# Down matmuls by pairs of experts, value products in halves, and a first mixer that starts with index scores and selection

## The reference, cut to what matters

```python
# layer 0 mixer: pool branch and sparse attention (DSA)
u, q, k, v, qi, ki, wi = jnp.split(hn @ w_in, ...)          # 512,512,128,128,256,64,4 columns
a_out = pool_mix(concat(pool_hist, u), ...)                 # windows 2,4,8,16, then one 128x128 product each
s_idx = sum over 4 index heads of relu(qi . ki) * wi        # index scores
sel   = top_k(where(admitted, s_idx, NEG_INF), n_sel)       # 128 keys (prompt), 72 (sample)
b_out = softmax over the selected keys, 8 heads             # 'bthd,bshd', then p @ v
y     = concat(a_out, b_out) @ w_out
# layer 1 mixer: stick-breaking attention (8 heads) and differential attention (4 heads)
# every layer: mixture of experts, 16 experts, each token goes to 2 of them
for e in range(16):
    hid = silu(x @ w1[e]) * (x @ w3[e])                     # 1024 -> 512
    y = y + gate[:, e:e + 1] * (hid @ w2[e])                # 512 -> 1024
```

## Time and profile before

| | us |
|---|---|
| median of 3 runs | 1469.23 (1467.95 to 1471.14) |
| the profiled execution | 1469.25 |
| its span in the trace | 1467.3 |
| PE busy in the span | 1286.9 (88%) |
| DVE, ACT, POOL busy | 469.3, 290.7, 165.4 |

### The profile page before, as it was taken

The page is one execution under the profiler, slowest core; times in us unless marked ns, Lnnn a source line. Parts: engine busy times, 40 slices in busy tenths (PEclk is TensorE's granted clock), DMA queues, the critical chain, the costliest instruction groups (busy, mean ns, idle before and its releaser), DMA issues.

```text
span 1467.3 us, 27763 instructions
## 1 busy us (share of the span) xinstructions
PE 1286.9 (88%) x11991; PEld 825.1 (56%) x11991; DVE 469.3 (32%) x1130; ACT 290.7 (20%) x703; POOL 165.4 (11%) x216
## 2 busy tenths in 40 slices
PE   6999789959999999948998799989877999999960
PEld 3454345548777777714444444444537777777740
DVE  3057873251000000025346651274542000000007
ACT  2122423210000000012345530242210000000013
POOL 0133100010000000020112221110001000000014
PEclk8997979969999999978999799999877999999995
DMA  9400100069999999772002201030038999999744
GB/s 287 129 10 5 59 1 29 15 230 348 372 371 382 380 379 363 293 240 101 22 15 77 107 15 43 29 119 15 29 102 300 385 375 383 381 381 363 306 136 151
DMA packets 69320, 283.55 MB, mean 193 GB/s; under 512 B 19181, under 2 KB 20253, under 8 KB 61002
## 3 DMA queue, kind: packets, MB, share of 16 engines
q1 hardware_dynamic: 56190, 237.94, 43.9%
q0 software_dynamic: 9216, 31.11, 6.0%
q10 hardware_dynamic: 3788, 12.65, 2.2%
HBM read 257.20 MB, written 24.48 MB: 192 GB/s over the span
## 4 chain that ended last, share of the span: by engine, by line
PE 75%; DVE 11%; issue 6%; DMA 2%; ACT 2%; POOL 2%; POOLq 0%; ACTq 0%; DVEq 0%; SPq 0%
PE bank L1058 24%; PE bank L781 15%; PE bank L1070 14%; PE bank L984 8%; PE bank L931 2%; PE bank L814 2%; PE bank L1043 2%; PE bank L900 2%; DVE slot L1546 1%; POOL slot L1985 1%; DVE h L1846 1%; PE bank L909 1%; DVE stats L1545 1%; PE bank L804 1%; DVE stats L1451 1%
## 5 line engine op out<-in xcount | busy, mean ns | idle before, releaser
L1058 PE MATMUL bank<-arena,slot 128*64 128x96 f32 x8192 | 351.4, 248 | 4.5 <-issue 4.4
L1058 PEld LDWEIGHTS bank<-arena,slot 128*64 128x64 f32 x8192 | 343.6, 138 | 11.0 <-issue 8.2
L781 PE MATMUL bank<-slot,xT 128*128 128x512 f32 x512 | 243.8, 633 | 1.1 <-issue 0.9
L1070 PE MATMUL bank<-slot,arena 128*96 128x512 f32 x512 | 227.4, 597 | 2.4 <-ACT arena L1345 2.4
L781 PEld LDWEIGHTS bank<-slot,xT 128*128 128x128 f32 x512 | 102.3, 205 | 122.9 <-issue 122.3
L1070 PEld LDWEIGHTS bank<-slot,arena 128*96 128x96 f32 x512 | 80.8, 163 | 126.8 <-issue 123.3
L1830 DVE TENSOR_TENSOR arena<-arena,bank 128x384 f32<-128x384 f32 x32 | 17.7, 554 | 353.8 <-ACT arena L1338 353.8
L984 PE MATMUL bank<-slot,normed 128*128 128x512 f32 x256 | 119.1, 620 | 0.2 <-ACT normed L1308 0.2
L1822 DVE TENSOR_TENSOR arena<-bank,params 128x768 f32<-128x768 f32 x32 | 30.6, 958 | 191.2 <-PE bank L1043 191.2
L1338 ACT ACTIVATE arena<-bank 128x384 f32<-128x384 f32 x32 | 15.7, 491 | 366.2 <-PE bank L1058 366.2
L931 PE MATMUL bank<-arena,slot 128*128 128x64 f32 (+5 forms) x520 | 78.4, 284 | 4.6 <-ACT slot L1247 3.7
(11 more groups left out here) (179 smaller groups left out, 1105.4 us busy)
## 6 DMA issues: line engine op xcount, KB each, us to landing
slot<-in_moe_w SPq DMA_DIRECT2D x96, 2048.0 KB, 13.3
expert_rows<-arena ACTq DMA_DIRECT2D x32, 384.0 KB, 8.6
slot<-in_w_in_odd SPq DMA_DIRECT2D x6, 2048.0 KB, 9.9
slot<-in_w_in_even SPq DMA_DIRECT2D x3, 2048.0 KB, 15.9
slot<-in_w_out_even SPq DMA_DIRECT2D x2, 2048.0 KB, 10.2
normed_rows<-slot POOLq DMA_DIRECT2D x8, 512.0 KB, 2.9
out<-arena POOLq DMA_DIRECT2D x16, 256.0 KB, 2.3
slot<-in_w_out_odd SPq DMA_DIRECT2D x2, 2048.0 KB, 7.9
```

What stands on the lines that cost most here:

```text
L781: last = nc.tensor.matmul(b[o:o + wide, 0:n], xT[:, k, P * t + o:P * t + o + wide], w[:, k, 0:n], start=(k == 0), stop=(k == KC - 1))
L1058: last = nc.tensor.matmul(bank[o:o + 64, b, CAP * m:CAP * m + CAP], weights(w[par])[:, k, at_:at_ + 64], xgT[:, par, k, :], start=(k == 0) ...
L1070: last = nc.tensor.matmul(bank[0:CAP, 6 + j, :], ghid[:, par, m, :], weights(W2[par], 4)[:, m, 512 * j:512 * j + 512], start=(m == 0), sto ...
```

## The change

Three things.

**Down matmuls by pairs.** Two experts' 2 x 96 = 192 rows are six thirds of 32 rows; times two column halves that is 12 pieces. A *wave* takes four of them at once, each in its own group of 32 columns of the array and with its own moving w2, so that a pair takes three waves of 4 x 4 matmuls. The first wave of a pair goes behind the odd expert's up, the other two behind the next even expert's. A wave fills one bank (6 or 7 in turn); ACT copies 128x512 and stores it with two DMAs of 2-KB rows. w2 gets a third buffer (in `xT`), and SP's order of loads changes: at an even expert e, w2(e+1) and w2(e+2) are issued behind w13(e+2), so that w2(14) now stands ahead of w13(15).

```diff
+WAVES = (((0, 0, 0), (0, 1, 0), (0, 2, 0), (0, 0, 1)),          # (expert of the pair, third, half)
+         ((0, 1, 1), (0, 2, 1), (1, 0, 0), (1, 1, 0)),
+         ((1, 2, 0), (1, 0, 1), (1, 1, 1), (1, 2, 1)))
-            def down(l, e, par):
-                for j in range(2):
-                    for m in range(4):
-                        last = nc.tensor.matmul(bank[0:CAP, 6 + j, :], ghid[:, par, m, :],
-                                                weights(W2[par], 4)[:, m, 512 * j:512 * j + 512],
-                                                start=(m == 0), stop=(m == 3))
+            def down(l, p, part):
+                for m in range(4):
+                    for c, (q, third, j) in enumerate(WAVES[part]):
+                        w2 = w2_ring[(2 * p + q) % 3].rearrange("p (k n) -> p k n", k=4)
+                        last = nc.tensor.matmul(bank[QUARTER * c:QUARTER * c + QUARTER, 6 + w % 2, :],
+                                                ghid[:, q, m, QUARTER * third:QUARTER * third + QUARTER],
+                                                w2[:, m, 512 * j:512 * j + 512], start=(m == 0), stop=(m == 3))
...
                     up(l, e, e % 2)
-                    if e > 0:
-                        down(l, e - 1, (e - 1) % 2)
-                down(l, NE - 1, (NE - 1) % 2)
+                    if e % 2:
+                        down(l, e // 2, 0)
+                    elif e > 0:
+                        down(l, e // 2 - 1, 1)
+                        down(l, e // 2 - 1, 2)
+                down(l, NE // 2 - 1, 1)
+                down(l, NE // 2 - 1, 2)
...
+                    w2_ring_load(l, 2)
+                    for e in range(NE):
+                        if e + 2 < NE:
+                            sp.wait_ge(up_done[l], e + 1)
+                            w13_load(l, e + 2, e % 2)
+                        if e >= 2 and e % 2 == 0:
+                            for done in (e - 2, e - 1):
+                                if done + 3 < NE:
+                                    sp.wait_ge(down_done[l], last_wave(done))
```

**Value products in halves.** For the 128-row tiles of DSA and stick-breaking each matmul becomes two, with 64 columns of probabilities as weights, in the two halves of the array:

```diff
+                    wide = r if w == P else min(r, 64)
                     for i, (vb, kr) in enumerate(blocks):
-                        last = nc.tensor.matmul(out[0:r, w * hd:w * hd + w], probT[0:kr, n % 2, i, 0:r],
+                        for o in range(0, r, wide):
+                            last = nc.tensor.matmul(out[o:o + wide, w * hd:w * hd + w],
+                                                    probT[0:kr, n % 2, i, o:o + wide],
```

```diff
+    dsa(0, "q")
+    dsa(0, "kT")
+    out.append(("us",))
+    dsa(1, "kT", "qiT")
+    dsa(0, "qT")
+    dsa(1, "ix0", "ix1", "ix2", "ix3")
+    out.append(("S", 1, 0, 8))
+    dsa(2, "kv", "ki")
+    out.append(("S", 1, 8, 16))
+    dsa(1, "q")
+    out.append(("u", 0))
...
+    for t in range(2):
+        merged(extra, {(t, hd): [("S", t + 2, 2 * hd, 2 * hd + 2)] for hd in range(8)})
+    merged(extra, {(2, hd): [("S", 4, hd, hd + 1 if hd < 7 else 9)] for hd in range(8)})
...
+                   (0, 3): project("dsa", 4, "cache"), (0, 4): [("u", 1)], (0, 5): project("dsa", 4, "kv4"),
...
+                   (3, 3): [("Ub", 3), ("y", 0, 0, 0)], (3, 4): [("O", "dsa", 2)],
...
-            w_out_load(w_out_even, OUT_EVEN, (lambda: sp.wait_ge(bank_filled, number[("us",)] + 1),
+            w_out_load(w_out_even, OUT_EVEN, (lambda: sp.wait_ge(bank_filled, number[("u", 3)] + 1),
```

More of the change, by code:

```diff
@@ L1 @@
+import itertools
 import concourse.bass as bass
@@ L122, in schedule @@
-    extra = {}
[L123 to L132, removed]
@@ L133, in schedule, with turn_in, dsa @@
-    merged(extra, {(0, 0): project("dsa", 1, "qT"), (0, 1): [("Uv", 0), ("Us", 1)], (0, 3): [("Ub", 0)],
[7 rows of a table removed]
+    def turn_in(kind, *tiles):
+        out.extend((kind, 0, t) for t in tiles)
+    def dsa(t, *items):
+        out.extend(project("dsa", t, *items))
+    turn_in("N", 0, 1)
+    turn_in("X", 0)
+    turn_in("N", 2)
+    turn_in("X", 1)
+    turn_in("T", 0)
+    turn_in("N", 3)
+    turn_in("T", 1)
+    turn_in("X", 2)
+    dsa(0, "kv")
+    turn_in("X", 3)
+    turn_in("N", 4)
+    dsa(0, "ki")
@@ L189, in schedule @@
             out.extend([("X", 4, t - 1), ("Z", t - 1)])
-    placed, due, open_pair = [], [], False
+    placed, due = [], []
     for step in out:
-        while due and (step[0] == "router" or len(placed) >= due[0][0] and not open_pair):
+        while due and (step[0] == "router" or len(placed) >= due[0][0]):
             placed.append(due.pop(0)[1])
         placed.append(step)
-        if step[0] == "A":
-            open_pair = step[1] != "diff" and step[2] % 2 == 0 and step[2] < NT * HEADS[step[1]]
         if step[0] == "T" and step[1] in (1, 3):
@@ L243, in bank_plan, with read_order @@
     return plan
+def read_order(steps, plan):
+    held, out = [], []
+    todo = iter(plan)
+    for step in steps:
+        mine = [key for key, _ in itertools.islice(todo, len(bank_plan([step])))]
+        if step[0] == "A" and step[1] != "diff":
+            t, hd = divmod(step[2], HEADS[step[1]])
+            held += [k for k in mine if k[1] == "s"]
+            out += [k for k in held if k[2:4] == (t, hd)]
+            held = [k for k in held if k[2:4] != (t, hd)]
+            mine = [k for k in mine if k[1] != "s"]
+        out += mine
+    return out
 def stream_kernel(nc, x_prompt, x_sample, cache_pool, cache_dsa_k, cache_dsa_v, cache_idx_k, cache_sb_k,
@@ L257, in stream_kernel @@
     rank, last_rank = {}, {"act": 0, "dve": 0}
-    for key, who in plan:
-        last_rank[who] += 1
-        rank[key] = last_rank[who]
+    for key in read_order(steps, plan):
+        last_rank[reader[key]] += 1
+        rank[key] = last_rank[reader[key]]
     ctx = ExitStack()
@@ L397, in stream_kernel @@
         lam_tmp = crow[:, 1, 0:HD]
-        histrow = ropeA
-        us_parts = rows[:, 0:512]
+        poolout = crow[:, 0, :]
+        us_parts, histrow = (mixT[:, g, 0:512] for g in (2, 3))
         PARTS = {"kv": 0, "k": 0, "v": 1, "q": {"dsa": 1, "sb": 0, "diff": 0}}
@@ L426, in stream_kernel @@
         w13_in = [[sem(f"{q}_w13_in{l}") for q in ("even", "odd")] for l in range(2)]
-        w2_in = [[sem(f"{q}_w2_in{l}") for q in ("even", "odd")] for l in range(2)]
+        w2_in = [[sem(f"w2_in{l}{r}") for r in range(3)] for l in range(2)]
         gfin_in = sem("gfin_in")
@@ L534, in xn @@
             return xn_of[n][:, t % 3, :]
+        rope_at = {}
+        for kind, *a in steps:
+            if kind == "P" and a[2] in ("kv", "k", "q") and a[0] != "sb":
+                rope_at[a[0], a[1], int(a[2] == "q")] = len(rope_at)
         def rope_no(mech, t, part):
-            return (0 if mech == "dsa" else 2 * NT) + 2 * t + part
+            return rope_at[mech, t, part]
         def rows2d(ap):
@@ L645, in experts @@
                     w2_load(l, 1, 1, first)
[L646 to L663, removed]
+                    w2_ring_load(l, 2)
[7 more added lines that the diff above has]
+                                    sp.wait_ge(down_done[l], last_wave(done))
+                                    w2_ring_load(l, done + 3)
                     sp.wait_ge(up_done[l], NE - 1)
@@ L805, in transposes, with step_u, step_us @@
                 last.then_inc(bank_filled, 1)
-            def step_u():
+            def step_u(f):
+                b = fill(("u", f))
                 pe.wait_ge(slot_in[S_U], 16)
[L809 to L816, removed]
+                xT_ready(0, 3)
+                for k in range(KC):
+                    last = nc.tensor.matmul(b[:, :], weights(S_U)[:, k, P * f:P * f + P], xT[:, k, 0:SEQ],
+                                            start=(k == 0), stop=(k == KC - 1))
+                last.then_inc(bank_filled, 1)
+            def step_us():
+                pe.wait_ge(slot_in[S_U], 16)
+                xT_ready(0, NT - 1)
                 project_parts(("us4",), weights(S_U))
@@ L1357, in experts, with step_u, step_us @@
                         own_silu(l, e)
-                        if e > 0:
-                            own_rows(l, e - 1)
-                    own_rows(l, NE - 1)
-            def step_u():
-                for f in range(4):
-                    b = filled(act, ("u", f))
-                    read(nc.scalar.copy(uT[:, f, HIST:HIST + SEQ], b))
+                        if e % 2:
+                            own_rows(l, e // 2, 0)
+                        elif e > 0:
+                            own_rows(l, e // 2 - 1, 1)
+                            own_rows(l, e // 2 - 1, 2)
+                    own_rows(l, NE // 2 - 1, 1)
+                    own_rows(l, NE // 2 - 1, 2)
+            def step_u(f):
+                b = filled(act, ("u", f))
+                read(nc.scalar.copy(uT[:, f, HIST:HIST + SEQ], b))
+            def step_us():
                 b = filled(act, ("us4",))
@@ L2033, in own_tokens @@
                         .then_inc(xg_in[l][e % 3], 16)
-                for r in range(2):
```

(3 more changed lines are left out.)

161 lines of the change are left out of this document (102 added, 59 removed), and 12 rows, old and new, of tables (at, index).

## The result

The change takes 1415.27 us (median of 4 runs, 1413.67 to 1415.94) where the kernel before takes 1469.55: a ratio of 0.9629, 95% interval [0.9612, 0.9646], 54 us less. The forecast was 1423, 46 less, with 1399 to 1447 as its range.

A forecast was written before the change was run, and what follows sets the result against it. PE and DMA were taken to run level in the experts, with DMA becoming the bound after the change; experts 29.6, first mixer 14.0 and second mixer 3 sum to 46.6 us off 1469.25, giving 1423, range 1399 to 1447.

The forecast's parts named there:

- PE's side of the pairs: Experts: three waves of 3.64 us, 10.9, replace two downs of 14.08, 3.2 us less per pair if PE alone limits.
- the tail: End of each layer's experts, PE alone: 16.4 us after up(15) becomes 11.4, a gain of 5.0.
- The switches between group shapes: PE changing between turns, up and waves: 0 to 0.4 us each, at most 0.8 per pair, hidden under DMA's floor.
- DMA's pace: Experts: DMA moves 385 GB/s, so a pair takes 36.8 us, 0.44 less than before.
- the recorded step: Layer 0's experts: up(15) starts as its weights land, at 598.2 instead of 608.0, 9.8 us earlier.
- The lead: Experts: weights land 12.1 us before up(15); used up at 2.8 per pair, so DMA bounds after some five pairs.
- the sign forecast for the trace: Experts: PE idle ahead of up from about the fifth pair, DMA share 1.0 at 380 to 390 GB/s.
- The first rival: Experts: DMA keeps up and PE stays the bound, 27.4 us less per layer, 1397 in all; chance 0.14.
- w2(14) ahead of w13(15): End of each layer's experts: 2.097 MB ahead of the last weights delay their landing by 5.4 us.
- Halves: Value products in 64-row halves: 72 ns less per block, 5.8 us in the first mixer, 3 in the second.
- The first mixer's start: First projection starts at about 12.3 instead of 20.70: 8.4 us earlier, of which 2.4 go to later transposes.
- My layout: First mixer laid out engine by engine: end 14.3 us earlier, PE waits 44.5 old, 43.2 new, first output product about 190.

The follow-up runs named there:

- The moved steps: Changed kernel with tile 0's key transposes ahead of its q projection and the sample tile's transposes behind it: 1411.16 us; with w2(2)'s load also moved, 1410.24.

## Why the prediction was right or wrong, point by point

*PE's side of the pairs* was right. A wave takes 3.57 us (3.64 from the sample tile's row), the tail 11.1 from the last up to the end of the last copy (11.4), before 16.3 (16.4). The switches between group shapes show no idle; the turn behind a wave takes 1.06 in the chain, 0.86 behind a down, and that 0.2 per turn is within the bounds given. In the kernel before the one turn behind an up, at 344.18, takes 1.06 too. For the rule on draining in TensorEngine Tiling (Array Packing), Key Properties (the Trainium skill), this is the only trace of a price here, and no run shows that the switch is its cause.

*DMA's pace* was the step that failed in size: 385 GB/s and 36.8 us a pair, measured 396 to 398 and 35.3 to 35.5. I took the highest rate of a kernel whose PE asked for 380, and read a share of 0.99 as a limit. With 397 a pair takes 14.16 MB / 397 = 35.7 us, and the loads of expert 15 would land at 595.9 - 7 x 1.5 + 5.3 = 590.7 on the old time axis. Measured from the first up (331.00 before, 320.57 after) they land 260.5 us in, before 264.9: 4.4 earlier, where the recorded step has 2.3 later and the new pace 5.2 earlier.

*The lead* was to be used up by about the fifth pair, and it was, in the sixth. In layer 0 the weights of experts 3, 5, 7, 9, 11, 13 and 15 land 6.7, 3.3, 1.8, 0.9, 0, 1.5 and 2.3 us ahead of their up. PE waits for weights twice, once at up(2), which the forecast didn't have, and once at up(11) (timeline of PE):

```profile
353.63 10.82 PE L1135 MATMUL bank<-arena,slot 128*64 128x96 f32 x256 [0.89 <-DMA slot<-in_moe_w]
...
514.41 12.43 PE L1135 MATMUL bank<-arena,slot 128*64 128x96 f32 x256 [1.98 <-DMA slot<-in_moe_w]
```

Layer 1 has the same two waits, 2.04 and 1.37. So the sign forecast for the trace, gaps of PE with DMA at a share of 1, is there, but small; and up(15), which was to start as its weights land, starts 2.3 and 2.1 us behind that, so that PE, not DMA, was the end of each layer. From the first up to the start of up(15) the change gains 14.2 and 12.8 us where the sum has 9.8. The first rival (PE stays the bound) didn't hold either: a layer gains 20.5 and 18.1 us, between the forecast's 14.8 and the rival's 27.4.

*w2(14) ahead of w13(15)* was priced at 5.4 and cost nothing. Such a price is paid only where DMA is the bound at that moment.

*Halves*: a block gains 57 ns in the chain, not 72, and not everywhere. I let all 5.8 us of the first mixer count, because PE's work counts where PE is busy, and half of them in the second. In the first mixer about two thirds of the blocks lie ahead of the first output product, in the stretch that holds PE's waits for DVE, and there no gain can be told; behind it they gave 2.6. The 3 us of the second mixer are neither shown nor ruled out by these traces.

*The first mixer's start* was right: the first projection starts at 12.63 in the chain (forecast 12.3), released by the w_kv load.

```profile
2.16 10.43 DMA slot<-in_w_in_even
...
12.63 8.67 PE bank L850 x48
...
199.01 7.10 PE bank L1061 x16
```

Its waits were not. My layout had the first output product at 190; it came at 199.01, and at 197.0 to 198.1 in three more traces of this order. The moved steps bring it to 192.7 and 192.4, so that 4 to 6 of those 7 to 9 us hang on the two waits named above. The layout had the steps that make them, with a row's duration each; it had PE's q at 6.92, where it ran for 9.84, with a granted clock of 0.50 (the lower level, 1.2 GHz) from 35 to 39 us, right behind the wait of 2.98. The loads of w_out were no part of it: issued at 175.9, landed at 190.3, with the product at 199.0. As two errors of the first mixer (halves and waits) had one sign and DMA's pace the other, the sum came out within 8 us: that closeness is in part luck.

## What to carry to other kernels

A DMA share of 0.99 beside an engine that never waits told here that both run level, not what DMA could move; to learn its limit, make the engine faster or the load smaller and look at GB/s per share. A price for a load that stands ahead of another counts only where the second one's landing is what an engine waits for, so look up the lead (landing to use) at that place, under the new pace. Time that an engine saves ahead of a stretch bounded by another engine can be lost in it, and what it saves behind the last such wait stays: of the halves nothing showed ahead of the first output product and some 2.6 us behind it. The same stage can differ by 5 us between two traces, as here; compare several traces before a gain is given to a stage.

## What the runs showed of the hardware that was not expected

In the experts DMA moved 378 GB/s at a share of 0.99, 323 at 0.86, 396 at 1.01 and 347 at 0.90: 376 to 392 GB/s per unit of share, so that the busy share is itself no fixed measure of a rate. The measured 396 to 398 lie above the 358 per core that DMA: Bandwidth & Descriptors, section "Where 436 GB/s comes from" (the Trainium skill), gives for HBM, and below its ceiling of 435. Which of several causes sets them (gathers, stores of 2-KB rows, or the loads themselves) was not tried.
